# Differential attention: inverse, product and sum at row ends each one score read apart, and the minimum over a row's maxima behind the next read

## What is computed

```python
def blk(qp, q1b, q2b):
    mask = _chunk_mask(qp, kpos)
    dist = jnp.abs(qp[:, None] - kpos[None, :]).astype(f32)
    bias = jnp.where(mask[None], -slopes[:, None, None] * dist[None], NEG)
    s1 = jnp.einsum('bhqd,bhkd->bhqk', q1b, k1).astype(f32) * scale + bias
    s2 = jnp.einsum('bhqd,bhkd->bhqk', q2b, k2).astype(f32) * scale + bias
    a = jax.nn.softmax(s1, axis=-1) - lam * jax.nn.softmax(s2, axis=-1)
    return jnp.einsum('bhqk,bhkv->bhqv', a.astype(v.dtype), v)
```

## Time and profile before

| | |
|---|---|
| runs | 2601.49, 2602.57, 2603.08 us; median 2602.57 |
| profiled execution, span | 2600.7 us (its own time is not given apart; the median lies 1.9 us over the span) |
| TensorE busy | 2540.5 us (98%) |
| VectorE busy | 1614.7 us (62%) |
| ScalarE busy | 1212.5 us (47%) |
| GpSimd busy | 332.0 us (13%) |
| differential attention | some 432 to 773 us, and its last transposes and products behind |
| granted TensorE clock | 0.997 of full speed in the mean |

### The profile page before, as it was taken

How to read it: one execution, slowest core, us unless ns; L and a number is a source line. 1 busy time by engine, 2 the same in 40 slices (tenths; PEclk the granted TensorE clock), 3 DMA queues, 4 the chain that set the end, 5 groups by cost and what they waited for, 6 DMA issues and landing times.

```text
span 2600.7 us, 35372 instructions
## 1 busy us (share of the span) xinstructions
PE 2540.5 (98%) x12220; PEld 2114.9 (81%) x12220; DVE 1614.7 (62%) x3499; ACT 1212.5 (47%) x2183; POOL 332.0 (13%) x368
## 2 busy tenths in 40 slices
PE   8999999999999999999999999999999999999997
PEld 7998888777667999977877888888888888888886
DVE  6123306998995776654458677876757465564765
ACT  6112314777764555554544333533335353443554
POOL 1110002222221222210000000000000001111143
PEclk9999999999999999999999999999999999999999
DMA  7334458553332111135677767657655365776787
GB/s 232 122 106 125 126 163 253 143 135 87 93 131 90 36 31 45 41 110 158 194 247 220 221 200 237 218 182 216 190 161 179 110 221 108 171 167 162 203 162 137
DMA packets 329436, 398.59 MB, mean 153 GB/s; under 512 B 21408, under 2 KB 235664, under 8 KB 320944
## 3 DMA queue, kind: packets, MB, share of 16 engines
q1 hardware_dynamic: 311696, 364.41, 44.7%
q0 software_dynamic: 17568, 31.99, 8.4%
HBM read 239.86 MB, written 156.48 MB: 152 GB/s over the span
## 4 chain that ended last, share of the span: by engine, by line
PE 62%; DVE 3%; DMA 1%; ACT 1%; issue 1%; SPq 0%; POOL 0%; DVEq 0%; ACTq 0%; POOLq 0%
PE ff_ps_x L3262 26%; PE ff_ps_m L3262 13%; PE ff_ps_z L3262 6%; PE ml_ps_s L2139 6%; PE ff_ps_m L1695 4%; PE ml_ps_o L2168 4%; PE ml_ps_t L2152 2%; DMA ml_v_raw<-scr_yT 1%; DMA ff_pieces<-scr_acc 0%; PE ff_ps_r L2699 0%; PE mo_ps_t L2716 0%; SPq L2326 0%; DVE ff_pieces L2429 0%; DVE ff_pieces L2620 0%; DVE ff_pieces L2616 0%
## 5 line engine op out<-in xcount | busy, mean ns | idle before, releaser
L3262 PE MATMUL ff_ps_x<-ff_mv_hi_p,ff_st_hi_p 128*128 128x512 f32 x764 | 297.8, 390 | 0.5 <-ACT ff_u L3002 0.5
L3262 PE MATMUL ff_ps_x<-ff_mv_hi_p,ff_st_lo_p 128*128 128x512 f32 x764 | 297.3, 389 | 0.0
L3262 PE MATMUL ff_ps_x<-ff_mv_lo_p,ff_st_hi_p 128*128 128x512 f32 x764 | 297.2, 389 | 0.0
L2139 PE MATMUL ml_ps_s<-wide,ml_qs 128*128 128x416 f32 (+14 forms) x880 | 195.6, 356 | 3.7 <-PEq L137 2.7
L3108 DVE TENSOR_TENSOR ff_st_lo_p<-ff_ps_m,ff_st_hi_p 128x512 fp32r<-128x512 f32 x190 | 130.8, 689 | 103.4 <-ACT ff_st_hi_p L2985 103.4
L2952 POOL DMA_DIRECT2D scr_acc<-ff_pieces x64 | 55.5, 872 | 1015.3 <-DVE ff_pieces L3132 946.9
L3002 ACT ACTIVATE ff_u<-ff_ps_x 128x512 f32<-128x512 f32 x128 | 76.6, 598 | 215.0 <-PE ff_ps_x L3262 215.0
L3262 PEld LDWEIGHTS ff_ps_x<-ff_mv_hi_p,ff_st_hi_p 128*128 128x128 f32 x764 | 143.4, 188 | 32.4 <-issue 2.0
L3262 PEld LDWEIGHTS ff_ps_x<-ff_mv_hi_p,ff_st_lo_p 128*128 128x128 f32 x764 | 143.4, 188 | 29.9
L3262 PEld LDWEIGHTS ff_ps_x<-ff_mv_lo_p,ff_st_hi_p 128*128 128x128 f32 x764 | 143.4, 188 | 29.6
L2139 PEld LDWEIGHTS ml_ps_s<-wide,ml_qs 128*128 128x128 f32 x880 | 152.0, 191 | 16.3 <-issue 2.9
(11 more groups left out here) (318 smaller groups left out, 6349.7 us busy)
## 6 DMA issues: line engine op xcount, KB each, us to landing
st_raw<-in_w_ff SPq DMA_DIRECT2D x64, 512.0 KB, 6.2
scr_hid<-ff_pieces SPq DMA_DIRECT2D x128, 256.0 KB, 2.7
st_raw<-scr_hid SPq DMA_DIRECT2D x64, 512.0 KB, 5.4
ring<-in_w_ff SPq DMA_DIRECT2D x28, 1024.0 KB, 7.7
scr_t<-ring SPq DMA_DIRECT2D x24, 1024.0 KB, 5.8
ring<-scr_t SPq DMA_DIRECT2D x21, 1024.0 KB, 8.1
scr_acc<-ff_pieces POOLq DMA_DIRECT2D x64, 256.0 KB, 4.1
ring<-scr_u SPq DMA_DIRECT2D x13, 1024.0 KB, 8.4
```

What stands on the lines that cost most here:

```text
L2139: m = pe.matmul(ps_s[n % NSB][:, 0:w], q, k, start=j == 0, stop=j == len(pairs) - 1)
L3262: m = pe.matmul(bank[:, :], w[kind][:, k], a[kind][:, k], start=start and k == 0 and i == 0, stop=stop and k == KH - 1 and i == 2, skip_gr ...
```

## The change

In the order of steps the minimum becomes a step of its own, `max`, put one chunk behind the row's last chunk. `end` is split: `inverse` where `end` was, `ratio` (the product with minus lambda) one chunk behind it, `end` (the row's product alone) two chunks behind it. `ratio` and `end` of a row may now pass the row end behind it and must be done by the one after. VectorE gets one more wait, before the first chunk of a second component, for the product of the row two before, whose buffer it overwrites. `cost` is as it was, so that the cost of an `end` now counts two chunks later, and turns and products shift with it.

```diff
+        def row_of(step):
+            return step[2] - NT * step[1]
+
+        def followers(due):
+            return [(left, (kind, *step[1:])) for step in due if step[0] == "inverse" for left, kind in ((1, "ratio"), (2, "end"))]
...
-                    steps += [step for left, step in later if left <= 0]
-                    later = [(left, step) for left, step in later if left > 0]
+                    due = [step for left, step in later if left <= 0]
+                    steps += due
+                    later = [(left, step) for left, step in later if left > 0] + followers(due)
                     if k0 + w == META + P * (i + 1):
-                        steps += [step for _, step in later if step[2] - NT * step[1] < i]
-                        later = [(left, step) for left, step in later if step[2] - NT * step[1] >= i]
-                        later.append((1, ("exp", 0, i, c)))
+                        due = [step for _, step in later if row_of(step) < i - (step[0] in ("ratio", "end"))]
+                        steps += due
+                        later = [(left, step) for left, step in later if step not in due] + followers(due)
+                        later += [(1, ("max", 0, i, c)), (1, ("exp", 0, i, c))]
                         if c == 0:
                             later.append((SCALE_AFTER, ("scale", 0, i)))
                         if c == COMPS - 1:
-                            later.append((END_AFTER, ("end", 0, i)))
+                            later.append((END_AFTER, ("inverse", 0, i)))
...
+                if c == 1 and k0 == 0 and not (first_head and i < 2):
+                    dve.wait_ge(probs_ready, NT * h + i - 1)
...
+            def inverse(h, i, u, **at):
+                dve.wait_ge(exp_ready, NT * COMPS * h + COMPS * (i + 1))
+                dve.reciprocal(inv[:, i % 2, 1:2], total[:, i % 2, 1:2]).then_inc(inv2_step, 1)
+
+            def ratio(h, i, u, **at):
...
+                dve.wait_ge(inv2_step, 2 * (NT * h + i) + 1)
+                dve.tensor_scalar(inv2[:, i % 2:i % 2 + 1], inv[:, i % 2, 1:2], lam[:, 3:4], None, ALU.mult).then_inc(inv2_step, 1)
+
+            def end(h, i, u, **at):
+                dve.wait_ge(inv2_step, 2 * (NT * h + i) + 2)
+                dve.wait_ge(first_scaled, NT * h + i + 1)
```

More of the change, by code:

```diff
@@ L1534, in chunk, with row_max @@
                                          accum_out=mx[:, i % 2, c, nth:nth + 1]).then_inc(scores_read, 1)
-                if k0 + w == META + P * (i + 1):
-                    dve.wait_ge(scores_read, NCH * h + n + 1)
-                    dve.tensor_scalar(nmax_all[:, 0:nth + 1], mx[:, i % 2, c, 0:nth + 1], -scale, None, ALU.mult, ALU.min,
-                                      accum_out=nmax[:, i % 2, c:c + 1]).then_inc(max_ready, 1)
                 if first_head and n == 1:
                     lambda_sums()
+            def row_max(h, i, c, **at):
+                n = max(m for m in range(NCH) if chunks[m][:2] == (i, c))
+                parts = sum(1 for chunk in chunks if chunk[:2] == (i, c))
+                dve.wait_ge(scores_read, NCH * h + n + 1)
+                dve.tensor_scalar(nmax_all[:, 0:parts], mx[:, i % 2, c, 0:parts], -scale, None, ALU.mult, ALU.min,
+                                  accum_out=nmax[:, i % 2, c:c + 1]).then_inc(max_ready, 1)
             def lambda_sums():
@@ L1563, in invert @@
                 dve.reciprocal(inv[:, i % 2, 0:1], total[:, i % 2, 0:1]).then_inc(inv_ready, 1)
-            def end(h, i, u, **at):
+            def inverse(h, i, u, **at):
+                dve.wait_ge(exp_ready, NT * COMPS * h + COMPS * (i + 1))
+                dve.reciprocal(inv[:, i % 2, 1:2], total[:, i % 2, 1:2]).then_inc(inv2_step, 1)
+            def ratio(h, i, u, **at):
                 if isinstance(h, int) and (h, i) == (0, 0):
                     minus_lambda()
-                n = 2 * (NT * h + i)
-                dve.wait_ge(exp_ready, NT * COMPS * h + COMPS * (i + 1))
-                dve.reciprocal(inv[:, i % 2, 1:2], total[:, i % 2, 1:2]).then_inc(inv2_step, 1)
-                dve.wait_ge(inv2_step, n + 1)
+                dve.wait_ge(inv2_step, 2 * (NT * h + i) + 1)
                 dve.tensor_scalar(inv2[:, i % 2:i % 2 + 1], inv[:, i % 2, 1:2], lam[:, 3:4], None, ALU.mult).then_inc(inv2_step, 1)
-                dve.wait_ge(inv2_step, n + 2)
+            def end(h, i, u, **at):
+                dve.wait_ge(inv2_step, 2 * (NT * h + i) + 2)
                 dve.wait_ge(first_scaled, NT * h + i + 1)
@@ L1577, in end @@
                                          op0=ALU.mult, op1=ALU.add).then_inc(probs_ready, 1)
-            heads(dve, {"chunk": chunk, "scale": invert, "end": end})
+            heads(dve, {"chunk": chunk, "max": row_max, "scale": invert, "inverse": inverse, "ratio": ratio, "end": end})
             dve.wait_ge(probs_ready, NT * H)
```

## The result

| | before | after |
|---|---|---|
| median of the timed runs, 10 of each on one chip, us | 2600.66 | 2607.08 |
| lowest and highest, us | 2598.54 to 2603.08 | 2604.09 to 2607.83 |
| profiled execution, span, us | 2600.7 | 2605.6 |
| last product of probabilities and values starts at, us | 799.06 | 805.58 |

The changed kernel is slower: ratio 1.0025, 95% interval 1.0016 to 1.0033, so 6.4 us. The forecast was 2604.3 with 2594.5 to 2614.0, and "within 0.2%" as the likeliest case; 0.25% lies just above it. The stage ends 6.5 us later; as its first score starts 0.3 us sooner (431.93 for 432.20), it is 6.8 us longer. The span is only 4.9 longer.

The account below looks back on a forecast made before the run. The prediction took the stage as bound by two nearly full engines, TensorE and VectorE, waiting for each other. Terms -6.1, +1.6, +2.2 and +4.0 gave +1.7 us: span 2602.4, time 2604.3 us, range 2594.5 to 2614.

Parts of the forecast that it names:

- within 0.2%: Whole kernel: time the same as before to within 0.2%, chance 0.48 over all cases.
- The drains: VectorE: 256 removed dependences (128 minima, 64 lambda products, 64 row products) at 0.119 us each save 30.5 us.
- the drains stay: Rival on VectorE: small operations cost their 0.2 us wherever they stand, the 30.5 us stay; 2622 us, chance 0.05.
- VectorE's stands for the exponential: VectorE before inverses: later exponentials make it wait 5.3 us a head, 21 in all; signs: some 45 waits, near 20 us.
- (a): Between heads, three times: row 15's product ends 0.5 us later and TensorE's transposes wait for it, +1.6 us.
- (b): Right behind the head handover, three times: TensorE's first product waits 0.7 us more for ScalarE's copy, +2.2 us.
- (c): Row 11 to group 2, four times: TensorE waits 1.0 us for the row product two reads later, +4.0 us.
- TensorE's idling for unread banks, all of it given back: TensorE before scores: its waits for banks not yet read vanish, -6.1 us.
- VectorE's negative balance: VectorE over the stage: -30.5 for drains, -2.8 for GpSimd waits, +21 for exponential waits, -12 us.
- Copies come later, and I cost this at nothing: ScalarE's copies behind the second component's exponential come half a microsecond a row later; TensorE three banks behind, cost nothing.
- the handover of a row decides: Slower rival: row product two reads later, bank waits all stay, 1.5 us each at (c); 2612.4 us, chance 0.25.
- Each head as long as before within 1 us: Sign in the profile after: each head from the second on keeps its length within 1 us.

Follow-up runs that it names:

- the fourth experiment: Changed kernel with the minimum one read late only for first components of rows 3 to 15, at the row's end elsewhere; 2600.6 us, ratio 1.0005.
- the first experiment: Changed kernel with the minimum back at the row's end; inverse, lambda product and row product stay one read apart; 2598.03 us, 0.9993 of the kernel before.
- e4_min_c0: The fourth experiment: changed kernel with the minimum one read late only for first components of rows 3 to 15; 2600.6 us, ratio 1.0005.

## Why the prediction came out as it did

The time, 2607.1, was inside the range and 2.8 us above the forecast; the likeliest case, within 0.2%, was missed by 0.05%. That nearness is in part luck: the sum stood on a median of 2602.57 for the kernel before, and beside the changed kernel it measured 2600.66. As a change, +1.7 us was forecast and +6.4 came, and errors of both signs are in the sum. By its steps:

- **The drains, 30.5 us of VectorE: right.** Idle before the minimum 4.4 to 0.0, before the lambda product 2.3 to 0.0, waits for GpSimd 2.8 to none. What they are worth is less sure: the trio late in one piece against the trio late and apart gives 6.8 us of kernel time for 15.2 us of VectorE, part of it by the clock. The rival "the drains stay" is out in this kernel: the lambda product at 604.49 starts together with the accumulator read in front of it. The forecast took the Trainium skill (VectorE: DVE Perf Modes, section "The DRAIN you can't avoid") to say that every operation waits for an empty pipe; the same section adds that a next operation that is not held (made to wait until every earlier one has finished) starts earlier. This trace agrees: the independent product at 604.49 starts 0.08 us before the recorded end of the accumulator read.
- **VectorE's stands for the exponential, 21 us more: right in size.** They went from 6.7 to 24.1 us by 775 us, 37 times. The forecast has two figures that don't fit together: 21 us more in its sum, and near 20 in all, in some 45 waits, among its signs. This cancels what hiding the minima's drains saved: 15.5 us of these stands go when the minima go back (24.1 to 8.6), against 128 x 0.119 = 15.2.
- **(a) Row 15's product, +1.6: too high.** The three waits are 1.26, 1.62 and 1.27 for 3 x 1.26 before: +0.4. The product did come later, from its row's minimum by 0.5 us at the first and the third handover and by 0.8 at the second, the one shown above; there the minimum lies 6.0 us before the transposes (601.42 to 607.46) for 5.2. But 0.35 us of it TensorE had already lost on a bank: 1.10 at 600.32, for 0.75 in the profile before, at

```profile
597.15 0.63 PE L1609 MATMUL da_ps_s<-da_keys,ahead_q 128*128 128x400 f32 x2 [0.75 <-DVE da_mx L1531]
```

The sum had three handovers and the stage has four: the wait for row 15 of the last head grew by 0.8 us (2.78 to 3.60).
- **(b) The copy behind it, +2.2: near where it was looked for, missed elsewhere.** 0.48 became 0.96 three times, +1.4 in place of 2.2; the first head has one of 1.25 of which the sum had nothing (at 463.85; before, TensorE stood 1.07 us for a bank at 463.63). Together +2.7.
- **(c) Row 11, 4 x 1.0: right.** 0.88, 1.23, 0.88 and 0.88, together 3.9. Taking row 11 alone back removed all four, and 2.6 us of the median.
- **"TensorE's idling for unread banks, all of it given back": this step failed.** The ones inside a head went, 3.1 us, but 3.3 us stand there: three waits of 1.1 at a head's end. Before there were four of 0.74 at this place. Row 14's product of 1936 columns (597.47 to 599.70) holds up the reads in one piece. Taking small operations off its front does not make it shorter. The argument from VectorE's negative balance over the whole head was the error: a wait is caused in a place, by one operation of 2.2 us, and a balance says nothing of it.
- **"Copies come later, and I cost this at nothing": this failed too.** The cover was three banks of transposes; but ScalarE also empties the outputs, and the product of the next group's tile waits for that copy: 2.5 us in 4 waits, none before. The late minima of first components alone make it (2.5 us in the fourth experiment, 0.9 without them).

Taken together, the late minimum stands in the sum with 2.2 us on TensorE's path, and the first experiment gives 9 us for it. The late row product stands there with 5.6, and the trio late in one piece gives 4.8.

The forecast's +1.7, with +3.3 for the banks, +2.5 for the output copy, +0.5 for (b), -1.2 for (a) and -0.1 for (c), is +6.7, and TensorE's waits up to 775 us give +6.6. With the last head's row 15 and the half clock behind it they are +8.6, for a stage 6.8 us longer. The rival "the handover of a row decides" had the right sign; its 2612.4 needed (c) at 1.5 us and all of the 6.1 to stay. Its cause, the row product two reads later, is only part of it: with that alone, and the minimum at the row's end, the kernel is no slower than before (2598.0). "Each head as long as before within 1 us" was off: 88.27 us for the third, 1.8 more: 0.36 at row 15's product, 0.48 at the copy, 0.63 and 0.88 new, less 0.1 for banks. The five add up to 2.3; 0.5 us of it was made good elsewhere in the head.

What stays open is how much the hidden drains are worth by themselves, since no pair of kernels differs in them alone clear of the noise; and how the 5 us of the late minima of the middle rows split up, of which the output copies are 1.7 (2.6 for 0.9) and the first head's copy 1.3. That the span is only 4.9 us longer needs no cause in the change: the time outside the stage ranges from 2230.5 to 2234.8 us over the thirteen profiles (2233.8 before, 2232.0 after).

## What to carry to other kernels

Hiding the drain between two dependent small operations behind a long independent one works, but each such step moves its result one long operation later. Do it for a result that nobody waits for (here the lambda product), and not for one that another engine waits for at once (here the minimum, which starts ScalarE); and try the last row before a handover in one piece: at row 11 this removed the waits and some 2.6 us, at row 15 it brought nothing. When two edits of an order are combined, look at what now stands in front of the most urgent step: the minimum behind the whole trio cost 68 us, behind the separated one 9. And price waits of the other engine one by one, from the operation that causes each, never by the balance of an engine over a stretch.

## What the runs showed of the hardware that had not been expected

TensorE's granted clock takes part in these differences, and no list of waits shows it. In the profile of the trio late in one piece TensorE idles 1.4 us for a bank at the end of each of the first three heads, and the same ten passes of values follow each time:

```profile
513.18 3.81 PE L1680 MATMUL da_ps_o<-da_pT,da_v 128*128 128x512 f32 x10
...
600.48 5.38 PE L1680 MATMUL da_ps_o<-da_pT,da_v 128*128 128x512 f32 x10
...
688.37 5.51 PE L1680 MATMUL da_ps_o<-da_pT,da_v 128*128 128x512 f32 x10
```

The first time the clock is 1.00, that is 2.4 GHz. The second and the third time it falls to half, 1.2 GHz (0.50 from 600.4 to 602.9 and from 690 to 692), and the passes take 1.6 and 1.7 us longer. The first experiment's profile has no such fall before 774 us. An idle of this length does not always bring it: the 1.41 us in front of 512.31 did not, nor did 3.28 us before the last head's transposes in e4_min_c0, whose clock stays full through the stage. What decides is open.

Over executions of one kernel a lower clock goes with a longer time, 0.8 to 1.5 us for each 0.001 in the three groups of 27 of the kernel before. By this an estimated 1.3 to 2.3 of the 6.8 us between the trio in one piece and apart (clocks of 0.9959 and 0.9975) is the clock, and about 1 of the 4.8 us to before. Whether the late steps lower the clock, through the idle that they make, no run tests.

The weight loader's short waits before scores (0.24 us pieces in the earlier trace rows) were taken as no idle time of the array. That is not sure either. The same two kernels have nearly the same idle of TensorE, 15.4 and 15.9 us from 430 to 785 us, yet the stage in one piece is 4.8 us longer. The clock makes 1.9 of it (3.3 at the two handovers, less 1.4 at the end, where the other profile's fall is the longer one). The first head, up to its transposes, is 87.2 for 85.3 us with only 0.2 more of waits and a full clock in both. The loader differs, in one piece and then apart:

```profile
PEld da_ps_s L1633 <- DVE da_mx L1547: 23.1, 65, 1.6
```

```profile
PEld da_ps_s L1632 <- DVE da_mx L1546: 13.7, 44, 1.2
```

That these waits cost the missing 3 us is a guess; no run changed them alone.
